# A two-layer hybrid decoder trunk: the mixer phase in another order, with other sharing of buffers and the scores of two heads side by side

## The reference

```python
def reference(x, ...):
    for l in range(2):
        h = rms_norm(x, attn_pre_g[l])
        u = jnp.einsum('bsd,de->bse', h, w_in[l])
        u_conv, rq, rk, rv, rg, mq, mk, mv, u_pool = jnp.split(u, ...)
        y_a = conv_mixer(u_conv, ...)      # GLU, causal depthwise conv of 31 taps, LayerNorm, swish
        y_b = retention(rq, rk, rv, rg, ...)   # 4 heads of 64, chunks of 128, state carried on
        y_c = moba_attention(mq, mk, mv)   # causal attention; with 512 tokens all blocks are chosen
        y_d = pool_mixer(u_pool, ...)      # causal means over 2, 4, 8, 16 tokens
        y = jnp.einsum('bse,ed->bsd', jnp.concatenate([y_a, y_b, y_c, y_d], -1), w_out[l])
        x = x + rms_norm(y, attn_post_g[l])
        h = rms_norm(x, ffn_pre_g[l])
        f = jax.nn.silu(h @ w_gate[l]) * (h @ w_up[l])
        x = x + rms_norm(f @ w_down[l], ffn_post_g[l])
    return x
```

## Time and profile before

| | us |
|---|---|
| median of three runs | 1186.14 |
| lowest and highest | 1182.47, 1186.31 |
| the profiled execution | 1183.07 |
| its span in the profile | 1181.2 |
| PE busy | 1113.9 (94%) |
| DVE busy | 619.1 (52%) |
| ACT busy | 407.6 (35%) |
| mean granted clock of TensorE | 0.982 |

### The profile page before, as it was taken

One profiled execution on the slowest core, in us unless ns is written; L12 is line 12 of the kernel. 1 busy time (PEld: TensorE's weight loads), 2 busy tenths in 40 slices (PEclk: granted clock), 3 DMA queues, 4 the chain that ended last, 5 costly groups with the idle time before them and its releaser, 6 DMA issues. The chain is left out here.

```text
span 1181.2 us, 16609 instructions
## 1 busy us (share of the span) xinstructions
PE 1113.9 (94%) x6640; PEld 669.7 (57%) x6640; DVE 619.1 (52%) x1410; ACT 407.6 (35%) x808; POOL 4.9 (0%) x18
## 2 busy tenths in 40 slices
PE   2998989999999999999999798998999999999997
PEld 2886864578444444444488586654864444444443
DVE  6588886595333333322576887757753333332013
ACT  5424444454233333212234335443542233332001
POOL 1000000000000000000000000000000000000000
PEclk9998998999999999999999899998999999999998
DMA  7532221125334323333013241111443343223001
GB/s 255 173 109 92 89 72 36 37 82 168 107 108 138 98 90 103 107 107 107 1 55 126 74 141 37 36 37 36 143 143 107 107 125 101 98 92 103 1 18 54
DMA packets 57596, 109.64 MB, mean 93 GB/s; under 512 B 6960, under 2 KB 7216, under 8 KB 57392
## 3 DMA queue, kind: packets, MB, share of 16 engines
q1 hardware_dynamic: 57520, 108.58, 28.7%
HBM read 106.46 MB, written 2.10 MB: 92 GB/s over the span
## 5 line engine op out<-in xcount | busy, mean ns | idle before, releaser
L490 PE MATMUL ps<-hT,ring 128*128 128x512 f16 (+1 forms) x3264 | 549.1, 330 | 0.0
L490 PEld LDWEIGHTS ps<-hT,ring 128*128 128x128 f16 x3264 | 319.9, 98 | 224.1 <-issue 1.1
L490 PE MATMUL ps<-ring,U 128*128 128x512 f16 x1440 | 318.3, 381 | 0.0
L1116 DVE SCALAR_TENSOR_TENSOR ring<-raw,ring 128x512 f16<-128x512 f32 x376 | 235.7, 685 | 113.3 <-ACT ring L748 112.6
L748 ACT ACTIVATE ring<-raw 128x512 f16<-128x512 f32 x376 | 210.4, 621 | 141.0 <-PE ps L490 106.9
L490 PEld LDWEIGHTS ps<-ring,U 128*128 128x128 f16 x1440 | 141.6, 98 | 166.0 <-issue 3.0
L1401 DVE SCALAR_TENSOR_TENSOR R<-ps,R 128x512 f32<-128x512 f32 (+1 forms) x52 | 31.6, 609 | 263.6 <-ACT R L912 263.4
L490 PE MATMUL ps<-ring,hT 128*128 128x256 f16 x1152 | 139.0, 280 | 0.0
L912 ACT ACTIVATE R<-ps 128x512 f32<-128x512 f32 (+1 forms) x52 | 27.6, 530 | 284.6 <-PE ps L490 284.6
L490 PEld LDWEIGHTS ps<-ring,hT 128*128 128x128 f16 x1152 | 115.9, 101 | 16.3
L1204 DVE SCALAR_TENSOR_TENSOR E<-E,parx 128x256 f32<-128x256 f32 x240 | 101.3, 477 | 0.1
(11 more groups left out here) (95 smaller groups left out, 484.5 us busy)
## 6 DMA issues: line engine op xcount, KB each, us to landing
raw<-weights_dram SPq DMA_DIRECT2D x376, 256.0 KB, 3.4
gbc<-gains_dram SPq DMA_DIRECT2D x8, 512.0 KB, 5.9
xs<-x_dram SPq DMA_DIRECT2D x4, 512.0 KB, 5.4
out_dram<-xs SPq DMA_DIRECT2D x4, 512.0 KB, 2.6
cst<-consts_dram SPq DMA_DIRECT2D x1, 1296.0 KB, 7.7
bd<-pool_w_dram SPq DMA_DIRECT2D x8, 16.0 KB, 3.7
par<-params_dram SPq DMA_DIRECT2D x1, 76.0 KB, 5.8
cst<-consts_dram SPq DMA_DIRECT2D x1, 64.0 KB, 5.1
```

Of the source, the lines that this page charges most:

```text
L490: ins = mm(dst, st, mv_, start=first and i == 0, stop=last and i == 2, **kw)
L1116: V.scalar_tensor_tensor(out=ring[:, slot % RING, 1, raw_part(part)], in0=raw[:, n % NRAW, :], scalar=W_SCALE, in1=ring[:, slot % RING, 0, ...
```

## The change

Slots of W_in are renumbered so that attention's three come before the retention's, and go in three groups: 0 to 3 (both of the convolution, the queries and keys of attention), 4 to 7 (values of attention, then the retention's), 8 and 9 (pooling, retention gate). The first layer transposes only tiles 0 and 1 before its first unit, and tiles 2 and 3 between ticks, as the second does. `pr` and `pT` move to the buffer of the norm gains (`gbc`), which are then loaded later, when attention is through with it, so that attention and retention can overlap; the gate gets its own buffer `gt`; the convolution's norm gets its own columns beside the retention's. `moba_S` takes two heads in one call: both masks, then both score products. The W_out slots are taken in the order attention, convolution, retention, pooling. Ticks in `AT` and the lists of ACT and DVE are written anew. The very last product unit finishes its first 512 columns before its second, the last tile's mean of squares is made in two halves, and the output leaves in half tiles.

```diff
-CONV_A, CONV_G, RQ, RK, RV, POOL, MQ, MK, MV, RG = range(10)
+CONV_A, CONV_G, MQ, MK, MV, RQ, RK, RV, POOL, RG = range(10)
-IN_GROUPS = (range(0, 6), range(6, 10))
+IN_GROUPS = (range(0, 4), range(4, 8), range(8, 10))
...
-        ("pre_T", 2): 11, ("pre_T", 3): 28, ("ret_T", 0): 83, ("ret_S", 0): 89, ("ret_O", 0): 106,
...
+        ("pre_T", 2): 35, ("pre_T", 3): 46, ("moba_T", 0): 90, ("moba_T", 1): 113, ("moba_stage", 0): 117,
+        ("moba_stage", 1): 130, ("moba_T", 2): 154, ("moba_stage", 2): 157, ("moba_stage", 3): 171,
+        ("moba_stage", 4): 176, ("moba_stage", 5): 181, ("moba_Y", 0): 185, ("moba_T", 3): 192,
+        ("conv_T", 0): 193, ("moba_stage", 6): 208, ("moba_stage", 7): 218, ("ret_T", 0): 220,
+        ("conv_Y", 0): 223, ("ret_S", 0): 224, ("ret_O", 0): 230, ("ret_T", 1): 231, ("moba_stage", 8): 234,
+        ("ret_S", 1): 239, ("ret_O", 1): 243, ("moba_stage", 9): 245, ("moba_stage", 10): 256,
+        ("ret_T", 2): 256, ("ret_S", 2): 257, ("moba_stage", 11): 268, ("moba_Y", 1): 281, ("ret_T", 3): 294,
+        ("ret_Y", 0): 296, ("pool_Y", 0): 297, ("ret_O", 2): 298, ("ret_S", 3): 301, ("ret_O", 3): 306,
+        ("conv_T", 1): 311, ("conv_Y", 1): 326, ("ret_Y", 1): 341, ("pool_Y", 1): 350, ("fpre_T", 0): 371,
+        ("fpre_T", 1): 375, ("fpre_T", 2): 432, ("fpre_T", 3): 436, ("pre_T", 0): 948, ("pre_T", 1): 964,
...
-        pr_w, pT_w = carve(R, [2 * S, 2 * S])
+        pr_w, pT_w = gbc[:, 0, :], gbc[:, 1, :]
...
-                if at == PARTS * (OUT0 + 4) - 1:
-                    if l:
-                        sp.wait_ge(x_upd, yno("fpost", l - 1, NT - 1) + 1)
+                if at == PARTS * (GU0 + 3) - 1:
+                    sp.wait_ge(mPT_ps, ths(l, NT - 1, NH - 1))
                     gain_load(0, l)
-                    sp.wait_ge(xn_sb, xno("pre", l, NT - 1) + 1)
+                    sp.wait_ge(mPV, ths(l, NT - 1, NH - 1))
                     gain_load(3, l)
...
-                        pe.wait_ge((pool_y, conv_y, ret_y, moba_y)[n], hs(l, s))
+                        pe.wait_ge((moba_y, conv_y, ret_y, pool_y)[n], hs(l, s))
...
-            def moba_S(l, t, h):
...
-                b, r = (4, 6)[h % 2], rows_of(h)
-                take(b, mP, ths(l, t, h))
-                q = mqT[r, t % 2, h // 2, :]
-                mm(bank[b][:, tok(t)], ident16, neg16, start=True, stop=True)
-                mm(bank[b][:, 0:P * (t + 1)], q, mkT[r, h // 2, 0:P * (t + 1)], start=False, stop=True,
-                   skip_group_check=True).then_inc(mS_ps, 1)
+                for h in (h0, h0 + 1):
+                    b = (4, 6)[h % 2]
+                    take(b, mP, ths(l, t, h))
+                    mm(bank[b][:, tok(t)], ident16, neg16, start=True, stop=True)
+                for h in (h0, h0 + 1):
+                    b, r = (4, 6)[h % 2], rows_of(h)
+                    mm(bank[b][:, 0:P * (t + 1)], mqT[r, t % 2, h // 2, :], mkT[r, h // 2, 0:P * (t + 1)], start=False,
+                       stop=True, skip_group_check=True).then_inc(mS_ps, 1)
...
             pe.wait_ge(ident_in, 16)
-            for t in TILES:
+            for t in (0, 1):
                 h_T("pre", 0, t)
...
+            def gate(l, s):
+
+                dve.wait_ge(rg_th, hs(l, s))
...
+                V.scalar_tensor_tensor(out=gt, in0=th, scalar=1.0, in1=b256(unit_bank(RG, s)), op0=ALU.add,
+                                       op1=ALU.mult).then_inc(ret_g, 1)
```

The new lists of DVE around the middle of the phase and at its end, of which the prediction speaks (the numbers after `conv` are taps, `z` is the layer's first slot):

```diff
...
+                split_lo(z + 13)
+                conv(l, 1, 1)
+                lo_of(ybuf, conv_hi, 0, l, 0, 0.5 * A_SCALE, conv_y)
+                ret_mask(l, 1)
+                split_lo(z + 14)
+                ret_state(l, 1)
+                ret_rotate(l, 1, 0)
+                m_max(l, 3, 2)
+                ret_rotate(l, 1, 1)
+                m_norm(l, 2)
+                m_max(l, 3, 3)
+                ret_norm(l, 0, lambda: conv(l, 1, 1))
...
+                norm_y("post", l, 0)
+                lo_of(ybuf, pool_hi, 6, l, 1, A_SCALE, pool_y)
+                lo_of(rz, ret_hi, 2, l, 1, 0.5 * A_SCALE * UNSCALE, ret_y)
+                norm_y("post", l, 1)
+                norm_x("fpre", l, 0)
+                norm_x("fpre", l, 1)
+                h_lo_of("fpre", l, 0)
+                split_lo(z + 17)
+                h_lo_of("fpre", l, 1)
...
```

More of the change, by code:

```diff
@@ L121 @@
     {
[L122 to L126, removed]
@@ L134 @@
-    {
-        ("pre_T", 2): 11, ("pre_T", 3): 28, ("ret_T", 0): 83, ("ret_S", 0): 89, ("ret_O", 0): 106,
[L136 to L145, removed]
+        ("pre_T", 2): 55, ("pre_T", 3): 57, ("moba_T", 0): 101, ("moba_T", 1): 115, ("moba_stage", 0): 121,
@@ L712, in small_products @@
                 for t in (2, 3):
-                    if l and at == AT[l]["pre_T", t]: h_T("pre", l, t)
+                    if at == AT[l]["pre_T", t]: h_T("pre", l, t)
                 for s in range(2):
@@ L1150, in norm_y, with norm_out @@
                                        op0=ALU.mult, op1=ALU.add).then_inc(x_upd, 1)
+            def norm_out(t):
+                n = yno("fpost", L - 1, t)
+                final = t == NT - 1
+                r = rstd(t, (y_sq, n + 1 + final), 4 + t if final else None)
+                if t == 0:
+                    dve.wait_ge(gain_in[0], 16 * 2 * L)
+                for m in range(2):
+                    cols = slice(512 * m, 512 * (m + 1))
+                    src = bank[PAIR[t] + m][:, :]
+                    at = tick(V.scalar_tensor_tensor(out=src, in0=src, scalar=r, in1=gbc[:, 0, cols], op0=ALU.mult,
+                                                     op1=ALU.mult))
+                    after(at)
+                    V.scalar_tensor_tensor(out=xs[:, t, cols], in0=src, scalar=UNSCALE / RN, in1=xs[:, t, cols],
+                                           op0=ALU.mult, op1=ALU.add).then_inc(out_ready, 1)
             def norm_x(kind, l, t):
+                if l == L:
+                    return
                 n = xno(kind, l, t)
@@ new lines, in _ @@
+                norm_y("fpost", l - 1, 3)
+                zero(l)
+                norm_x("pre", l, 2)
+                norm_x("pre", l, 3)
+                glu(l, 0)
+                h_lo_of("pre", l, 2)
+                conv(l, 0, 1)
+                h_lo_of("pre", l, 3)
+                conv(l, 0, 4)
+                z = l * SLOTS
+                conv(l, 0, 6)
+                split_lo(z + 4)
+                moba_rotate(l, 0)
+                split_lo(z + 5)
+                conv(l, 0, 6)
@@ new lines, in _ @@
+                split_lo(z + 6)
+                conv(l, 0, 6)
+                glu(l, 1)
+                conv(l, 0, 4)
+                m_max(l, 0, 0)
+                conv(l, 0, 1)
+                m_max(l, 0, 1)
+                conv(l, 0, 9)
+                m_max(l, 0, 2)
+                conv(l, 0, 3)
+                split_lo(z + 7)
+                m_max(l, 0, 3)
+                moba_rotate(l, 1)
+                split_lo(z + 8)
+                conv(l, 0, 3)
+                m_max(l, 1, 0)
@@ L1521, in _ @@
-                lo_of(rz, ret_hi, 2, l, 1, 0.5 * A_SCALE * UNSCALE, ret_y)
-                conv_norm(l, 1)
-                split_lo(z + 16)
-                pool_windows(l, 1)
+                split_lo(z + 11)
+                conv(l, 1, 2)
+                ret_mask(l, 0)
+                conv_out(l, 0)
+                split_lo(z + 12)
+                ret_state(l, 0)
+                conv(l, 1, 4)
                 m_max(l, 3, 0)
                 m_max(l, 3, 1)
+                split_lo(z + 13)
@@ new lines, in _ @@
+                conv(l, 1, 1)
+                m_norm(l, 3)
+                conv(l, 1, 2)
+                pool_windows(l, 0)
+                conv(l, 1, 1)
+                lo_of(b256(5), moba_hi, 4, l, 1, A_SCALE, moba_y)
+                conv(l, 1, 12)
+                ret_state(l, 2)
+                conv(l, 1, 4)
+                ret_mask(l, 3)
+                gate(l, 0)
+                conv(l, 1, 2 * CW)
+                ret_out(l, 0)
+                conv_norm(l, 1)
+                lo_of(ybuf, pool_hi, 6, l, 0, A_SCALE, pool_y)
@@ L1530, in _ @@
+                lo_of(rz, ret_hi, 2, l, 0, 0.5 * A_SCALE * UNSCALE, ret_y)
+                ret_norm(l, 1)
                 conv_out(l, 1)
+                gate(l, 1)
+                split_lo(z + 15)
+                pool_windows(l, 1)
+                split_lo(z + 16)
                 lo_of(ybuf, conv_hi, 0, l, 1, 0.5 * A_SCALE, conv_y)
+                ret_out(l, 1)
+                norm_y("post", l, 0)
                 lo_of(ybuf, pool_hi, 6, l, 1, A_SCALE, pool_y)
-                m_norm(l, 3)
```

469 lines of the change are left out of this document (218 added, 251 removed).

## The result

| | before | changed |
|---|---|---|
| median of four runs, us | 1186.22 | 1109.51 |
| lowest and highest | 1182.47, 1186.39 | 1109.05, 1111.58 |
| the profiled execution, and its span | 1183.07, 1181.2 | 1109.05, 1107.2 |

The ratio is 0.9364, 95% interval 0.9342 to 0.9386. The change is 77 us faster. I forecast 50 us faster, and the time lies 2.5 us under my range.

The account below looks back on a forecast made before the run. PE was taken to bound the mixer phases by a small margin over DVE. From the span 1181.2: −22 (layer 0), −27.6 (layer 1), −1 (end) = 1130.6; plus 1.9 and 3.1 gives 1135.6, forecast 1136 us, range 1112 to 1169.

Parts of the forecast that it names:

- The start: Layer 0's first unit at 16.2 us, 12.8 earlier; tick 64 near 44; net gain there about 7 us.
- rival of 1166: Mixer phases keep losing 28 and 37 us; only start, pairs and end are won: 1166 us, chance 22%.
- The pairs: Attention scores of two heads side by side overlap, saving 5.9 us a layer (nothing to 6.7; 1.7 if only drains go).
- The new order: Reordered mixer phases with W_out: layer 0 228 instead of 249.8 us, layer 1 204 instead of 231.6.
- To that I add 8: Allowance in each layer's mixer phase: two waits with clock drops (3.4 and 1.7 us each), 4.6 for short waits.
- The walk of layer 1: Tick-by-tick estimate of PE and DVE through layer 1's mixer phase: 189 us of PE work plus 7 of waits, 196.
- 3 more for a late DVE: Layer 0's mixer phase: DVE about 3 us further behind than at the same tick of layer 1.
- Tight: Rival: the waits found and the allowance in the mixer phases both shrink to 4 us a layer; 1114 us, 15%.
- DVE lags: Rival: DVE's 171 us leave 18 us of slack in 189, PE loses as much as now; 1166 us, 22%.
- The clock rival: Hand-overs throughout both mixer phases hold the granted clock at 0.93, losing 28 us instead of 7; 1157 us, 8%.
- The rival on the other side: ACT stands for weight loads at eight split_hi a layer, delaying copies PE needs; up to 1202 us, 5%.
- The end: After the last product, halves overlap one square and let half the output leave earlier: gain 1 us, 0.5 to 2.

Follow-up runs that it names:

- after_fpre_early: The changed kernel with only the tick of tile 0's transpose before the feed-forward network moved earlier (371 to 367 and 361): 1116.23 us, ratio 0.9424.
- before_pairs: The kernel before with moba_S taking two heads side by side and nothing else changed: 1175.75 us, ratio 0.9944.
- after_gate_in_two: The changed kernel with the retention gate back in two steps without its own buffer, ret_Y of the second half and ret_out moved: 1120.92 us, ratio 0.9465.

## Why the prediction was right and wrong

**The bound** was right. PE bounds the new phases, and DVE is close behind: fewer taps bring nothing, and more work costs at once.

**The start.** 16.2 us was forecast for the first unit, 16.63 came; 44 for tick 64, 42.68 came. What it is worth depends on the order: 9 to 10 us in the new one, nothing kept at W_out's end in the old. My rival of 1166 counted it as if it added up.

**The pairs.** Forecast 5.9 us a layer; the trace gives 6.7, my upper value. The row of four retention heads was the better guide: with no full-array product between them the second head costs nothing. By the drain rule of the Trainium skill (TensorEngine Tiling, Key Properties) alone the estimate was 1.7. The trace agrees with its other half, that tiles of one mode work independently: 1.06 us for both heads.

**The new order: here the prediction failed.** The step is "To that I add 8", once for each layer. The walk of layer 1 itself ended at 196, and 193.9 came. On the walk I put two long waits with their clock drops and a sum for unseen short ones, because the kernel before had lost 28 and 37 us. Neither came. The clock stayed at 1.00, and PE is idle for 3.3 us of the phase in all, 1.9 of it in waits of over 0.5 us. In layer 0 the same 8 was added and 3 more for a late DVE: 228 forecast, 215.5 measured, a walk without them 217.3. Layer 1: 204 forecast, 193.9 measured. Together the phases are 22.6 us of the 26 by which the forecast was off. These allowances, 8, 8 and 3, are 19 of them; the walk's own error, 1.8 and 2.1, is most of the rest. The feed-forward stretches make 1.2. The step from the profiled span to the median, taken as 1.9 + 3.1, was 2.3 in the changed kernel and makes 2.7. The end came 0.4 us short of its 1.

The walk was nearer than its terms, and that is partly luck. It had 7 us of waits in layer 1, and 3.3 came. `ret_O` 1 doesn't wait there, stage 10 waits a tenth as long as forecast, and the longest wait, 1.37 us at stage 9, isn't in the walk. Against that PE's own work was put too low: 189 us, where 193.86 − 3.29 = 190.6 came although the pairs took 0.8 less than forecast.

The allowance was wrong in kind. Clock drops are not spread over a phase. In the trace of the kernel before they cost 8.5 and 10.2 us in the two layers, and all lie around six of the seven waits of over 2.1 us. In after_fpre_early one wait of 3.58 us brings the one drop of its phase. In the phases of the changed kernel no wait is longer than 1.4 us, and no drop came. So the loss of the old order says little about the new one. The price of one wait isn't fixed, though: 2.91 us at 102.39 in before_pairs cost no clock, and 1.12 us at 670.61 in after_gate_in_two cost 1.7.

**The rivals.** "Tight", 1114 at 15%, was the case that came, and the measured time was better still. "DVE lags" fits the old order in that its long waits are for DVE or ACT, but its reason was too simple: DVE's work in layer 1 is 171 us in both kernels and only its place differs. The clock rival, with the Trainium skill's micro-idles (TensorE: Matmul & The Clock Gate, "A second HAM failure mode"), didn't come true here: the stages stand at 1.00 with 13 waits of 0.16 to 1.10 us in layer 0's phase and 7 of 0.17 to 1.37 in layer 1's. The rival on the other side, ACT standing at weight loads, shows in PE's waits at one place of each layer, slot 13 ahead of stage 9, and cost 0.65 and 1.37 us.

**The end.** 1 us was forecast. The traces give 0.6 and the runs 0.8 to 1.8, within their scatter: open.

**What stays open.** That the order needs the sharing (attention's `pr` and `pT` out of the retention's buffer, the gate's own buffer, own columns for each norm) was tried for the gate alone, together with one moved tick and the moved `ret_out`. Attention and retention can't overlap with `pr` and `pT` in `R`, and a version of the new order without the overlap wasn't tried. How the 65 us divide between the order of slots, the ticks and the lists is not taken apart.

## What to carry to other kernels

Before adding an allowance for unseen waits to a walk of the queues, ask whether the losses of the old kernel were single long waits; if so, they and their clock drops go together. Here the walk alone, 217 and 196 us, was the better forecast. With a second engine near the bound, a wait that was removed at one product turned up at the next one fed by the same list: twice in the old order, and once in the new one. Single repairs brought nothing there that could be measured, and the order changed as a whole did. Idle time of the second engine is no measure of its slack: 25 us of idle held about 4.

## What the runs showed of the hardware

Two float32 products of 64 rows and 512 columns on the two halves of the array ran in 1.06 us, one of them alone in 1.05: the second was free. With a mask over all 128 rows between them the two took 2.41 us with their masks, instead of 1.27. A wait of PE of 2.18 us in the kernel before (194.84) was followed by about 10 us at the lower clock, one of 3.58 us in after_fpre_early by about 3.4 us. One exchange of two neighbours on ScalarE that shortened a wait of 1.4 us made the kernel 7 to 9 us slower.
